# End of a layer in a two-layer diffusion backbone: tiles closed one behind the other, gate broadcast moved ahead of the expert loop, first projection in eighths

## What is computed

```python
for l in range(2):
    u = LN(x) * (1 + scale1) + shift1                 # "ln1", then modulate
    h = u @ w_in                                      # first columns: the RWKV projection
    y = mixers(h)                                     # RWKV-7, differential attention, HGRN2
    x = LN(alpha * x + gate1 * (y @ w_out)) * w1 + b1
    v = LN(x) * (1 + scale2) + shift2
    x = LN(alpha * x + gate2 * PEER(v)) * w2 + b2     # the "close" of the layer
# PEER: per token 8 heads pick 16 of 16384 experts each; out = sum gate * gelu(v . U[e]) * V[e]
# in the last layer only the 512 latent tokens are closed and stored
```

## Time and profile before

| | us |
|---|---|
| median of 3 runs (5734.59 to 5741.89) | 5739.09 |
| the profiled execution, its own time | 5738.8 |
| span of its profile | 5737.0 |
| PE busy | 5117.8 (89%) |
| DVE busy | 3642.8 (63%) |
| ACT busy | 1400.0 (24%) |
| POOL busy | 1558.9 (27%) |
| mean granted TensorE clock | 0.94 |

### The profile page before, as it was taken

One profiled execution on the slowest core, in us unless ns is written; L12 is line 12 of the kernel. 1 busy time (PEld: TensorE's weight loads), 2 busy tenths in 40 slices (PEclk: granted clock), 3 DMA queues, 4 the chain that ended last, 5 costly groups with the idle time before them and its releaser, 6 DMA issues.

```text
span 5737.0 us, 63806 instructions
## 1 busy us (share of the span) xinstructions
PE 5117.8 (89%) x22682; PEld 3349.9 (58%) x22682; DVE 3642.8 (63%) x8046; ACT 1400.0 (24%) x3524; POOL 1558.9 (27%) x1540
## 2 busy tenths in 40 slices
PE   8899989988878999999997789989988768999997
PEld 4688555657644455555553478845566545656664
DVE  2654465546787887877675454454656777866655
ACT  1210133222574121111112211022322461111111
POOL 0000000000246565656561000000000155545552
PEclk9899899999889999999998789999889889999998
DMA  3000003314249999999995100001213269999996
GB/s 139 8 9 8 26 15 103 103 52 169 103 187 348 417 409 421 414 418 402 416 418 219 47 8 8 8 22 44 96 52 132 78 257 407 420 415 416 418 418 256
DMA packets 294045, 1191.38 MB, mean 208 GB/s; under 512 B 24800, under 2 KB 106976, under 8 KB 208224
## 3 DMA queue, kind: packets, MB, share of 16 engines
q0 software_dynamic: 92160, 671.13, 28.3%
q1 hardware_dynamic: 195808, 460.83, 21.8%
q10 hardware_dynamic: 5760, 55.33, 2.4%
HBM read 1135.81 MB, written 51.38 MB: 207 GB/s over the span
## 4 chain that ended last, share of the span: by engine, by line
PE 65%; DVE 15%; DMA 13%; ACT 3%; issue 2%; POOL 1%; ACTq 0%; DVEq 0%; SPq 0%; POOLq 0%
PE psum L540 64%; DMA arena<-in_ut 10%; DVE arena L1544 2%; DMA x_tokens<-in_uv,arena 1%; DVE arena L1907 1%; DVE x_tokens L1544 1%; DVE arena L1982 1%; DVE arena L1704 1%; DVE u_features L1550 1%; DMA arena<-in_uv,arena 1%; DVE arena L1553 1%; DVE arena L1702 1%; DMA arena<-gate_blocks 1%; ACT arena L1139 1%; DVE arena L1547 1%
## 5 line engine op out<-in xcount | busy, mean ns | idle before, releaser
L540 PE MATMUL psum<-arena 128*128 128x64 f32 (+4 forms) x8128 | 1383.7, 336 | 39.9 <-DVE arena L1907 23.9
L540 PE MATMUL psum<-u_features,weight_ring 128*128 128x256 f32 (+2 forms) x4672 | 1347.4, 440 | 13.4 <-DVE u_features L1550 6.8
L540 PEld LDWEIGHTS psum<-arena 128*128 128x128 f32 (+1 forms) x8128 | 981.6, 197 | 409.8 <-issue 303.1
L540 PEld LDWEIGHTS psum<-u_features,weight_ring 128*128 128x128 f32 x4672 | 881.4, 193 | 381.7 <-issue 177.5
L540 PE MATMUL psum<-u_features,arena 128*128 128x384 f32 (+1 forms) x2048 | 594.5, 445 | 69.2 <-DMA arena<-in_ut 60.6
L1522 POOL TENSOR_TENSOR arena<-consts 128x1 f32<-128x1 f32 x640 | 354.1, 553 | 1076.9 <-DVE y_features L1811 931.3
L540 PE MATMUL psum<-weight_ring,consts 128*128 128x512 f32 x1280 | 572.2, 594 | 5.5 <-DVE consts L1798 5.4
L540 PEld LDWEIGHTS psum<-u_features,arena 128*128 128x128 f32 x2048 | 400.1, 197 | 287.6 <-DMA arena<-in_ut 80.2
L1523 POOL DMA_INDIRECT arena<-in_uv,arena x358 | 538.8, 1505 | 101.5 <-POOL arena L1522 96.2
L1265 ACT ACTIVATE arena<-arena 128x1 f32<-128x1 f32 x640 | 129.8, 203 | 1737.6 <-DVE arena L1803 1736.0
L1803 DVE CUSTOM_DVE_ANT_0 arena<-arena,y_features 128x1024 f32<-128x1024 f32 x358 | 437.0, 1221 | 56.4 <-DMA arena<-in_uv,arena 55.2
(11 more groups left out here) (215 smaller groups left out, 5237.3 us busy)
## 6 DMA issues: line engine op xcount, KB each, us to landing
weight_ring<-in_ws SPq DMA_DIRECT2D x242, 512.0 KB, 3.5
weight_ring<-in_ut SPq DMA_DIRECT2D x128, 512.0 KB, 13.6
weight_ring<-in_uv SPq DMA_DIRECT2D x128, 512.0 KB, 18.5
arena<-in_ut SPq DMA_DIRECT2D x128, 512.0 KB, 22.3
arena<-in_uv SPq DMA_DIRECT2D x128, 512.0 KB, 12.6
gate_blocks<-arena ACTq DMA_DIRECT2D x20, 2048.0 KB, 7.7
arena<-gate_blocks SPq DMA_DIRECT2D x32, 768.0 KB, 34.5
arena<-gate_blocks SPq DMA_DIRECT2D x32, 512.0 KB, 29.5
```

Source lines behind the costliest of these rows:

```text
L540: return pe.matmul(o, w, x, start=first, stop=last, skip_group_check=True)
```

## The change

Eight things are changed together, in both layers where they apply:

1. `close(l)` replaces the phases: DVE, ACT and POOL run a staggered loop over the tiles, in the order closing(l) = FETCHED + DENSE. Normalising and the row w2 become one instruction ((x - mean) * w2, into CENT) and the inverse root and b2 another, so one pass over each tile is gone.
2. down_block(127) signals each dense tile on its own ("tile added").
3. The second gate is broadcast ahead of the expert loop, into banks 0 to 3; G2 and the rows w2, b2 (LNR2) get other places in memory.
4. In layer 0 the sums and squares of ln1 of layer 1, and its XN tiles, are made inside close.
5. The parameters of layer 1 are loaded at block 100 of layer 0's loop instead of at the start of layer 1.
6. x_back is issued in iteration 123 of SP's loop, ahead of load_down(126) and load_down(127).
7. The first RWKV projection follows the modulation in eighths, between the transposes, in banks 6 and 7.
8. The output is stored tile by tile; the reload of the constants waits for the last "final" and stands behind four weight pieces.

```diff
+            def closing(l):
+                return FETCHED[l] + DENSE[l]
...
+                    if m == BLOCKS - 5:
+                        sp.wait_ge(*at("slot summed", l, last_in_x[l]))
+                        sp.wait_ge(SEM["x_spilled"], 16 * (2 * l + 1))
+                        lo = tiles(l)[0] * D
+                        sp.dma_start(X[:, lo:NT * D], a["x_kept"][:, lo:NT * D]).then_inc(SEM["x_back"], 16)
+            for t in closing(DEPTH - 1):
+                sp.wait_ge(*at("final", DEPTH - 1, t))
+                sp.dma_start(out[:, t - CT, :], xv[:, t, :]).then_inc(SEM["stored"], 16)
...
+            def transpose_x(l, ts):
+                for k in range(KB + 1):
+                    if 3 <= k < KB:
+                        pe.wait_ge(*at("ln1 modulated", l, k - 3))
+                    for t in ts if k < KB else ():
+                        if k == 0:
+                            pe.wait_ge(*at("ln1 normed", l, t))
+                        ins = pe.transpose(turned(2 * (k % 3), t), XN[:, t * D + k * P:t * D + (k + 1) * P], ident)
+                    if k < KB:
+                        done(ins, "ln1 turned", l, k)
+                    if k:
+                        w = piece_ready() if k == 1 else piece_now()
+                        pe.wait_ge(*at("ln1 modulated", l, k - 1))
+                        for o, lo, hi in ((bank(6, 256, 512), 0, CTX), (bank(7), CTX, T)):
+                            ins = mm(o, w[:, (k - 1) * P:k * P], xt(k - 1, lo, hi), k == 1, k == KB)
+                piece_done(ins, "rwkv projected", l, 0)
...
+                for s in streams:
+                    broadcast(l, "gate2", [40], s, 2 * s)
                 pe.wait_ge(*at("gates evicted", l, len(DENSE[l]) * GROUPS - 1))
...
+            def close(l):
+                order, more = closing(l), l + 1 < DEPTH
+                for n in range(len(order) + (4 if more else 2)):
+                    if n < len(order):
+                        t = order[n]
+                        x, s = x_tile(t), G2[1 if t < CT else 0]
+                        if t in FETCHED[l]:
+                            y = total(FETCHED[l].index(t))
+                        else:
+                            i = DENSE[l].index(t)
+                            dve.wait_ge(*at("tile added", l, i))
+                            y = PS[:, i * D:(i + 1) * D]
+                        tt(MIX, y, s, ALU.mult)
+                        stt(x, x, ALPHA, MIX, ALU.mult, ALU.add, "fin input", l, t)
+                    if 2 <= n < len(order) + 2:
+                        tile_spread(l, "fin", order[n - 2])
+                    if 1 <= n < len(order) + 1:
+                        t = order[n - 1]
+                        tile_mean(l, "fin", t)
+                        stt(CENT[n % 2], x_tile(t), ST[:, 8 + t:9 + t], LNR2[0], ALU.add, ALU.mult)
+                    if 2 <= n < len(order) + 2:
+                        t = order[n - 2]
+                        dve.wait_ge(*at("rsqrt", "fin", l, t))
+                        stt(x_tile(t), CENT[(n - 1) % 2], ST[:, 16 + t:17 + t], LNR2[1], ALU.mult, ALU.add, "final", l, t)
+                    if more and 3 <= n < len(order) + 3:
+                        tile_mean(l + 1, "ln1", order[n - 3])
+                    if more and n >= 4:
+                        t = order[n - 4]
+                        tile_spread(l + 1, "ln1", t)
+                        dve.wait_ge(*at("rsqrt", "ln1", l + 1, t))
+                        ts2(XN[:, t * D:(t + 1) * D], x_tile(t), ST[:, 8 + t:9 + t], ST[:, 16 + t:17 + t], ALU.add, ALU.mult,
+                            "ln1 normed", l + 1, t)
```

More of the change, by code:

```diff
@@ L769, in down_block @@
                                  m == 0, m == BLOCKS - 1)
+                    if m == BLOCKS - 1 and i + 1 < len(DENSE[l]):
+                        hidden(ins, "tile added", l, i)
                 hidden(ins, "block added", l, m)
+                if m == BLOCKS - 1:
+                    marks[("tile added", l, len(DENSE[l]) - 1)] = marks[("block added", l, m)]
             def broadcast(l, what, firsts, s, b):
@@ L1145, in attn_columns, with tile_sum, tile_squares @@
                 return (QA if c < 4 else KA)[:, (c % 4) * T:(c % 4 + 1) * T]
+            def tile_sum(l, what, t, sq):
+                done(act.activation(sq, x_tile(t), ACT.Copy, accum_out=ST[:, t:t + 1]), what + " sum", l, t)
+            def tile_squares(l, what, t, sq):
+                act.wait_ge(*at(what + " mean", l, t))
+                done(act.activation(sq, x_tile(t), ACT.Square, bias=ST[:, 8 + t:9 + t],
+                                    accum_out=ST[:, 16 + t:17 + t]), what + " squares", l, t)
             def stats(l, what, ts, sq):
@@ L1151, in stats @@
                         act.wait_ge(*at(what + " input", l, t))
[L1152 removed]
+                    tile_sum(l, what, t, sq)
                 for t in ts:
[L1154 to L1156 removed]
+                    tile_squares(l, what, t, sq)
             def rwkv_decays(l, i):
@@ L1481, in _ @@
                 ts = tiles(l)
[L1482 removed]
+                for t in range(NT) if l == 0 else ():
                     rsqrt(ST[:, 16 + t:17 + t], "ln1", l, t)
```

133 lines of the change are left out of this document (61 added, 72 removed).

## The result

The changed kernel takes **5679.59 us** (median of 4 runs, 5676.73 to 5683.11) against 5736.84 (5732.41 to 5741.89) for the kernel before: ratio 0.9898, 95% interval [0.9886, 0.991]. The forecast was 5666 in a range of 5657 to 5684. So the sign and the range were right, and the size was not: 57 us instead of 72. The profiled executions stand 55.7 us apart in span (5737.0 and 5681.3).

The account below looks back on a forecast made before the run. PE and DMA (share 0.99) were taken to bound the expert loop, DVE the layer ends. 41.4 + 5.8 + 6.3 + 18.7 + 3.1 - 2.0 - 0.9 = 72.4 us off 5738.8 gave 5666.4, forecast 5666, range 5657 to 5684.

Parts of the forecast that it names:

- The closing of layer 0: End of layer 0: DVE starts without waiting for the gate and paces six tiles; last XN at 3142.5 against 3183.93, gain 41.4 us.
- The closing of layer 1: End of layer 1: DVE starts at 5688.96, last "final" at 5711.3 against 5730.0, gain 18.7 us.
- The start of a layer: First projection in eighths between transposes, PE setting the pace: gain 6.3 us in layer 0, 5.8 in layer 1.
- second rival: Layer starts: PE stays at half clock in the mixed stretch, 4.3 and 5.1 us lost, total 5688; chance 0.1.
- the 3.03 us that I carried over: Start of layer 1: the scalars for lambda, between last XN and modulation, take 3.03 us as before.
- x_back, 2.0 forecast: Last gathers of layer 1: the earlier copy of x costs 2 us, bounds 0 and 5.2; hidden in layer 0.
- fourth rival: End of layer 1's loop: x_back delays the last gathers by 5.2 us or twice that, 5669 to 5675; chance 0.13.
- The store, 3.1 forecast: End of program: one 512 KB tile lands in 3.5 us instead of 6.98 for the whole store, gain 3.1 us.
- The broadcast ahead of the loop: Second gate's broadcast before the expert loop: 0.9 us shows in layer 0, bounds 0 and 4; hidden in layer 1.
- The staggered loop: Layer closings: rival that DVE waits for ACT once per tile, 1.27 us each, 13 us in all, 5679; chance 0.1.
- SP was not held: Loop ends: rival that x_back's wait for a slot sum holds SP ahead of the down loads, 5740 or more; chance 0.02.
- The gain arrives: Loops: rival that the gain does not arrive, since DMA at 0.99 sets the loops, 5739; chance 0.02.

Follow-up runs that it names:

- late copies: The changed kernel with x_back issued behind the loop over blocks again in both layers: 5674.0 us, ratio 0.9889.
- five other profiles with the early copy: Changed kernel profiled again, and with last roots off GpSimd, undivided first projection, gate broadcast behind the loop, or recurrence filling: 5678.05, 5677.13, 5690.43, 5711.92, 5683.31 us.
- its neighbour: The changed kernel with x_back behind the loop, last layer's roots off GpSimd and small products on PE at the start of layer 1 only: 5669.11 us, ratio 0.9877.
- the fastest kernel: The changed kernel with x_back behind the loop, last layer's roots off GpSimd and small products on PE at both layer starts: 5661.77 us, ratio 0.987.

## Why the prediction was right, and where it was not

**The closing of layer 0, 41.4 forecast, 40.2 measured.** The mechanism and its pieces held: six tiles paced by DVE, inverse roots showing 0.80 each, ACT covered (one wait of 0.44), dense tiles in time. DVE waited 6.6 us in all (seven times 0.80, once 0.52, once 0.44) for the 5.8 that I had counted; the rest of the missing 1.2 are hand-overs of 0.03. (The 1.18 and 1.27 that I put down to the earlier trace rows are the spacing of ACT's sums and squares in the same trace; the rows show their busy time, 1.06 and 1.15.) The closing of layer 1 gave 18.1 for 18.7.

**The start of a layer, 6.3 and 5.8 forecast, 5.1 and 4.9 measured.** One eighth and one lot of transposes ran at half clock as priced. In the second profile of the changed kernel the clock rose sooner (transposes behind the first eighth 0.87 instead of 1.49 in layer 0, 1.01 in layer 1), and against the first profile of before it gives 6.45 and 5.6. So the size forecast lies within what one kernel does. The blocks at full clock took 1.95 us for 1.93. The second rival is refuted in both layers by the rows of 0.82 and 1.46. The Trainium skill, TensorE: Matmul & The Clock Gate, Part 4, has it that transposes don't count as busy for the full clock. In the mixture it did no harm. And the kernel before speaks against it: there PE did nothing but transposes from 3175.08 on, behind 59.87 us without work, and the granted clock rose from 0.50 at 3190 to 1.00 at 3193. The measurement decides.

**Not foreseen, 1.3 won:** ACT loads the table for the exponential of lambda (1.28, at 3139.30). Before, this stood between the last XN and the modulation; now it runs while DVE still works on the last tiles, and the 3.03 us that I carried over became 1.69.

**x_back, 2.0 forecast, 7.0 measured: the step that failed first.** It reads "I take 2, since the later gathers have more slack". The waits of before at slot 252 (1.26 for DVE, 0.25 for PE) were the sign that they have little or none. The late copies show the size: 27.2 us instead of 34.4. It is more than the 5.2 us of transfer that I had set as the bound: PE idled 4.41 us instead of 0.25, and behind that the clock was down and the product took 6.31 instead of 3.69, 6.8 us together. In the five other profiles with the early copy the loss is 5 to 6. My fourth rival named this mechanism, with 0.13; of the forecast's miss of 14 it makes 3 to 5. In layer 0 the copy cost nothing, as said: PE is busy 92 of 92 us from 3000 on.

**The store, 3.1 forecast, -0.65 measured: the step that failed second.** The last tile's store itself was quick, 2.6 us for the forecast 3.5; by the Trainium skill, DMA: Bandwidth & Descriptors, Anatomy of one DMA, which gives its formula for the path of GpSimd, an estimate for these 512 KB would be 3.2; this store went through SP, and the trace has less. But I priced the end of the program by the store alone. The row that I had not looked for is GpSimd's DRAIN of 8.64 us, which the long store had covered. Freed of it, the end comes 3.0 us after the last "final", at the price of 1.5 us in the closing for the root by another way.

**The broadcast ahead of the loop, 0.9 forecast:** its 32 products took 4.25 us and PE's wait for the gates (2.22) vanished. A wait of 2.97 for an activation came up two blocks later (0.26 at that place before). From the first of the last three lots of products ahead of the loop (1766.46 before, 1762.21 now) to the fifth down_block it took 72.1 and now 72.5 us, in the second profiles 71.6 and 73.0: 0.4 and 1.4 more, around the forecast.

**Rivals.** The staggered loop does not leak: no wait of DVE for ACT over 0.44. SP was not held: x_back was issued 0.4 us after load_down(125). The gain arrives.

**What stays open:** 2.7 us of layer 0, of which the broadcast is 0.4 to 1.4, and 3.6 of layer 1 were lost in loops whose other instructions did not change. Layer 1 wanders by as much in one kernel. In layer 0 the changed kernel repeats. Clock falls behind short waits do cost time there, but the kernel before has them too (0.98 over 190 to 590 us in both), so they don't explain why the changed one is longer. And the kernel with small products in both layers is 9 us faster in that stretch than its neighbour, with nothing changed there. That the moment at which a wait falls decides over the clock would fit; no run here shows it. The Trainium skill, TensorE: Matmul & The Clock Gate, Part 1, says that the point of the clock's rise varies between runs of one kernel. The two profiles of the changed kernel agree: at the start of layer 0 the rise came sooner in the second one, and its first copy 1.3 us earlier.

## What to carry to other kernels

Before a transfer is moved forward "behind the last load", look for the smallest wait that its neighbours already show there: a wait of 1.26 for a gather and of 0.25 behind it on PE meant that there was next to no slack, and a late product is paid twice if the clock falls as well. What a long last transfer covers (here a closing step of GpSimd) has to be looked up before the transfer is cut. At the end of a stage with several phases, first make ready what the first phase waits for (30 us here), then merge the phases (28 us with what moved along).

## What the runs showed of the hardware

- GpSimd's closing DRAIN lasted 8.64 us in both main kernels and with the late copies, where GpSimd took part in the last tiles, at whatever time it began. Where its last work was a gather, it lasted 16.3 us (from 5622.2), 11.5 us with the late copies besides, and 10.7 us in the fastest kernel. It delayed the end by 4.8 us where it began 1.3 us ahead of the last store's issue, and not at all where it was over before.
- A wait of 4.41 us of PE was followed by a product mostly at half clock (6.31 for 3.69), and waits of 3.9 to 4.4 in five other profiles by 5.3 to 6.6. A wait of 1.72 us inside dense work was followed by lower clock at one tile and not at others, in the same program.
- Transposes alone were followed by the full clock: 0.50 at 3190, 1.00 at 3193.
- A small f32 product of 128x128 shows as two matmul instructions of 0.12 us at full clock, 0.21 at half: 16 of them (8 products) took 1.95 and 3.41 us. Ahead of the first eighth of layer 1 they had brought the clock up; in the recurrence 12 of them lasted 2.94 us in a wait of 1.72.
